# Splitting w_out ahead of attention, loading the first q rows there, and moving two low parts to GpSimd in a Hymba-style encoder layer

## Chip, cores and metric

The kernel runs as one program on one core of a Trainium2 chip. The metric is the device time of one execution in microseconds; a time given for a kernel is the median of its runs.

## The reference

One encoder layer is applied to two sequences of 1024 tokens with model width 1024 (kept as 16 tiles of 128 rows). What matters here, for each sequence:

```python
h = layer_norm(x)
q, k, v, x_lru, y_lru = split(h @ w_in)           # 512, 128, 128, 512, 512 columns
q, k = rope(rms_norm(q)), rope(rms_norm(k))       # 8 query heads and 2 key heads of 64
attn = softmax(q k^T / 8) v                       # full, both directions
lru  = (scan_forward + scan_backward)(conv(x_lru)) * gelu(y_lru)
merged = concat(rms_norm(attn) * attn_out_g, rms_norm(lru) * lru_out_g)
h = layer_norm(alpha * h + merged @ w_out)        # w_out is 1024 x 1024
h = layer_norm(alpha * h + hierarchical_moe(h))   # 16 experts, 2 for each token
```

Everything is float32. The kernel gets float32 accuracy from matrix products by splitting each factor into a high part (rounded to fp32r) and a low part (the rest), and adding three products (`three_pass`, lines 122 to 124).

## The kernel before

There are five stages, each with its own set of semaphores and mostly its own block of five instruction streams: `project_xy`, `qkv_lru`, `attend`, `experts` (with the routing in front) and `combine`. A block ends with a barrier of all engines, and a set of semaphores ends with a clearing and another one (`semaphores`, line 243). Within a block each engine's order is written out by hand; engines meet only in semaphores. The change lies at the end of `qkv_lru` and in the start and the first tile of `attend`.

The end of `qkv_lru` is called the gap here. The projections and scans are over or nearly over, and TensorE (PE) multiplies w_out by the router's columns, so that the router's logits can be had from attention's output: w_out's eight blocks of 128 rows are loaded (SP, lines 886 to 903), each is transposed in pieces on PE (`turn_w`, 953), copied out of PSUM by ScalarE (ACT, `read_w`, 1091) and multiplied by the router's columns (`times_w`, 962); sixteen such steps n, with two buffers at each hand-over. Between them stand the last transposes of q and k (`back`, 987), two column sums of the squared LRU output (`sums`, 923, copied by ACT at 1185), and at the end the product is transposed once more (`turn_r`, 972; `read_r`, 1097; the copy to w_r at 1188). VectorE (DVE) does the last unit's scans and output (1212 to 1222), GpSimd (POOL) the low part of the last q and k rows (`split`, 1316 and 1317).

`attend` loops over 16 tiles of 128 queries, with 8 heads each. For head h, PE transposes the probabilities (1550), computes the scores of head h + 2 (1538, 1539), and after every second head multiplies by v (1564). ACT copies the transposed probabilities to their high part (`d_probs_t_hi`, 1669) and computes exp of head h + 1 (1652). DVE subtracts to get the low part (`d_probs_t_lo`, 1755) and reduces the maximum of head h + 2 (1731). From the second tile on PE also projects the tile before through w_out, in thirds, and the normalisation follows. POOL only applies the layer norm's gain and shift, from the third tile on.

The start of `attend`: SP loads the first two q tiles from DRAM, then the gains out_g, two w_out blocks into the buffers raw, and the rest; ACT makes the high part of v (1645); DVE makes the LRU norms (a chain of small instructions, 1735 to 1738), the first two maxima, then the router part of w_out times out_g (1746) and v's low part (1747). In the first tile each head h also prepares w_out block h: ACT multiplies raw by out_g into `d_wo_hi` (1676), DVE subtracts into `d_wo_lo` (1761), and SP then loads block h + 2 into the freed buffer (1500). The first projection, in tile 1, waits for all of them. In the first tile:

```python
if not post:                                                  # ACT, head
    act.wait_ge(raw_in[h % 2], 16 * (h // 2 + 1))
    act.activation(w_hi[:, h, 0:D], raw[h % 2], ACT.Copy, scale=out_g[:, h:h + 1]).then_inc(hi_made, 1)
if not post:                                                  # DVE, head
    dve.wait_ge(hi_made, h + 1)
    dve.scalar_tensor_tensor(w_lo[:, h, 0:D], raw[h % 2], out_g[:, h:h + 1], w_hi[:, h, 0:D].bitcast(F32), ...)
```

## Time and profile before

| | us |
|---|---|
| median of 3 runs (lowest, highest) | 1601.76 (1598.63, 1602.78) |
| the profiled execution | 1599.9 |
| its span, first to last instruction | 1598.1 |
| PE busy in it | 1444.6 (90%) |
| DVE, ACT, POOL busy | 1126.0, 928.1, 481.1 |
| `project_xy`, to about | 218 |
| `qkv_lru`, to | 485.4 |
| start and first tile of `attend`, to | 529.2 |
| the rest of attention, to about | 1070 |
| routing, experts and the last norm | 1598.1 |

The profile is of one execution, its times count from the span's start. A line number such as L1755 is one of the kernel before. In a timeline row the first number is the start, the second the length, and the bracket at its end the idle time of that engine just before, with what ended it. Several matmuls or activations are merged into one row (x8). PEclk is the granted TensorE clock: 1.00 is 2.4 GHz, 0.50 is 1.2 GHz.

### The profile page before, as it was taken

Reading aid. Unit: us, or ns where it says so; the run is one execution under the profiler, and the core shown is the slowest. Engines: PE = TensorE matmul, PEld = TensorE weight load, DVE = VectorE, ACT = ScalarE, POOL = GpSimd, SP = SyncE. Lnnn points to the kernel's source line nnn. Section 1 sums busy time; section 2 is a strip of 40 time slices with the busy share of each in tenths; the row PEclk is TensorE's granted clock in tenths of the full one; section 3 lists DMA queues with packets and bytes.
Section 4 is the critical chain, followed back from the end, with each engine's and each line's share of the span. In section 5 each row is a group of like instructions: output and inputs, shape, how many; then the busy total and the mean of one; then the engine's idle time right before and its main releaser. Section 6 shows DMA issues by size and latency. Waiting matters only on the chain. (4 is left out here: it accounts for less than half of the span.)

```text
span 1598.1 us, 30295 instructions
## 1 busy us (share of the span) xinstructions
PE 1444.6 (90%) x8945; PEld 1258.7 (79%) x8947; DVE 1126.0 (70%) x2198; ACT 928.1 (58%) x1624; POOL 481.1 (30%) x347
## 2 busy tenths in 40 slices
PE   6999989999996999999999999975899999999940
PEld 5999977777765899999999999963777788777820
DVE  8787547999977888888888888877444334444237
ACT  4444338788776666666666666633565445555325
POOL 1212124565440011111121111131454433555318
PEclk9999999999998999999999999996999999999965
DMA  8865641544454112111112121127798787786576
GB/s 290 297 229 195 231 144 70 192 165 151 166 174 163 52 61 79 60 59 59 61 67 92 65 73 60 47 96 239 230 277 251 205 246 189 216 266 151 110 228 256
DMA packets 126214, 250.09 MB, mean 156 GB/s; under 512 B 24498, under 2 KB 77746, under 8 KB 126132
## 3 DMA queue, kind: packets, MB, share of 16 engines
q1 hardware_dynamic: 94000, 160.97, 29.2%
q0 software_dynamic: 12528, 45.99, 12.3%
q10 hardware_dynamic: 19604, 42.09, 7.0%
q8 instruction: 45, 0.74, 0.2%
q14 instruction: 37, 0.30, 0.1%
HBM read 154.35 MB, written 94.67 MB: 156 GB/s over the span
## 5 line engine op out<-in xcount | busy, mean ns | idle before, releaser
L1755 DVE TENSOR_TENSOR d_probs_t_lo<-d_pt_ps,d_probs_t_hi 128x512 fp32r<-128x512 f32 x256 | 165.0, 686 | 63.6 <-ACT d_probs_t_hi L1669 62.0
L1669 ACT ACTIVATE d_probs_t_hi<-d_pt_ps 128x512 fp32r<-128x512 f32 x256 | 139.2, 596 | 95.6 <-PE d_pt_ps L1550 89.3
L1731 DVE TENSOR_REDUCE d_neg_max<-d_s_ps 128x1 f32<-128x1024 f32 x128 | 155.5, 1215 | 3.4 <-PE d_s_ps L1539 3.4
L122 PE MATMUL acc<-k_hi,wl_hi 128*128 128x256 f32 x512 | 145.8, 285 | 4.4 <-DVE k_lo L597 4.4
L1652 ACT ACTIVATE d_probs<-d_s_ps,d_neg_max 128x1024 f32<-128x1024 f32 x128 | 143.4, 1121 | 4.3 <-DVE d_neg_max L1731 4.3
L122 PE MATMUL e_a_ps<-up_hi,e_xt_hi 128*128 x336 | 137.1, 408 | 9.7 <-DVE e_xt_lo L2591 5.0
L123 PE MATMUL acc<-k_lo,wl_hi 128*128 128x256 f32 x512 | 144.9, 283 | 0.0
L124 PE MATMUL acc<-k_hi,wl_lo 128*128 128x256 f32 x512 | 144.9, 283 | 0.0
L1550 PE MATMUL d_pt_ps<-ident,d_probs 128*128 128x128 f32 x1024 | 132.9, 273 | 4.7 <-ACT d_probs L1652 3.2
L1564 PE MATMUL d_ot_ps<-d_probs_t_hi,d_v_split 128*128 128x256 f32 x512 | 127.4, 287 | 8.3 <-DVE d_probs_t_lo L1755 8.3
L123 PE MATMUL e_a_ps<-up_lo,e_xt_hi 128*128 x336 | 133.4, 397 | 0.0
L124 PE MATMUL e_a_ps<-up_hi,e_xt_lo 128*128 x336 | 132.3, 394 | 0.0
L1564 PE MATMUL d_ot_ps<-d_probs_t_lo,d_v_split 128*128 128x256 f32 x512 | 124.9, 282 | 0.0
L1550 PEld LDWEIGHTS d_pt_ps<-ident,d_probs 128*128 128x128 f32 x1024 | 116.9, 140 | 7.8 <-ACT d_probs L1652 6.5
L122 PE MATMUL d_m_ps<-d_wo_hi,d_m_hi 128*128 128x348 f32 x360 | 120.6, 335 | 0.0
L1538 PE MATMUL d_s_ps<-k_hi,d_q_tile 128*128 128x512 f32 (+1 forms) x256 | 112.0, 438 | 5.5 <-DMA d_q_tile<-q_dram 5.5
L123 PE MATMUL d_m_ps<-d_wo_lo,d_m_hi 128*128 128x348 f32 x360 | 115.8, 322 | 0.0
L124 PE MATMUL d_m_ps<-d_wo_hi,d_m_lo 128*128 128x348 f32 x360 | 115.6, 321 | 0.0
L1929 POOL TENSOR_TENSOR l_h_tile<-d_s_tile,l_ln_g_b 128x512 f32<-128x512 f32 x16 | 20.6, 1285 | 309.6 <-ACT d_s_tile L1702 291.9
L1564 PEld LDWEIGHTS d_ot_ps<-d_probs_t_hi,d_v_split 128*128 128x128 f32 x512 | 97.1, 190 | 15.4 <-issue 15.4
L2416 POOL DMA_INDIRECT xg<-h_dram,ix x43 | 42.1, 978 | 211.5 <-ACT e_yt L2543 119.7
L122 PEld LDWEIGHTS acc<-k_hi,wl_hi 128*128 128x128 f32 x512 | 98.3, 192 | 5.0 <-DVE k_lo L597 5.0
(414 smaller groups left out, 4089.3 us busy)
## 6 DMA issues: line engine op xcount, KB each, us to landing
up_raw<-in_exp_w SPq DMA_DIRECT2D x32, 1024.0 KB, 9.5
down_raw<-in_exp_w SPq DMA_DIRECT2D x16, 1024.0 KB, 14.1
d_h_tile<-h_dram SPq DMA_DIRECT2D x16, 522.0 KB, 4.8
h_dram<-v_all ACTq DMA_DIRECT2D x16, 512.0 KB, 3.2
ht_hi_dram<-k_hi ACTq DMA_DIRECT2D x8, 1024.0 KB, 4.3
ht_lo_dram<-k_lo ACTq DMA_DIRECT2D x8, 1024.0 KB, 6.7
d_q_tile<-q_dram SPq DMA_DIRECT2D x16, 512.0 KB, 4.3
h_dram<-l_h_tile SPq DMA_DIRECT2D x16, 512.0 KB
```

Of the source, the lines that this page charges most:

```text
L122: pe.matmul(out, lhs[0], rhs[0], start=first, stop=False)
L123: pe.matmul(out, lhs[0], rhs[1], start=False, stop=False)
L124: return pe.matmul(out, lhs[1], rhs[0], start=False, stop=last)
L1538: pe.matmul(out, q_t[u][:, h, :], k_hi[:, h // GQ, keys], start=True, stop=False)
L1550: last = pe.transpose(pt_ps[c][:, j, :], pr[h % 2][:, k * P:(k + 1) * P], ident[:])
L1564: last = pe.matmul(ot_ps[:, 0:2 * P], vs[:, s * TPS + k, h // GQ].rearrange("p c d -> p (c d)"), part[:, k].rearrange("p e t -> p (e t)"), ...
L1652: act.activation(pr[h % 2][:], s_ps[h % 2][:], ACT.Exp, bias=nm[:, u, h:h + 1], accum_out=rsum[:, u, h:h + 1]).then_inc(p_done, 1)
L1669: act.activation(pt_hi[:, c * HALF:(c + 1) * HALF, h % 2], pt_ps[c][:], ACT.Copy).then_inc(pth_done[c], 1)
L1731: dve.tensor_reduce(nm[:, u, h:h + 1], s_ps[h % 2][:], AX, ALU.max, negate=True).then_inc(nm_done, 1)
L1755: dve.tensor_tensor(pt_lo[:, part, h % 2], pt_ps[c][:], pt_hi[:, part, h % 2].bitcast(F32), ALU.subtract)\
L1929: pool.tensor_tensor(h1[:, part], s_t[u][:, part], g_b[:, part], ALU.mult).then_inc(hg_done, 1)
L2416: pool.indirect_dma_start(xg[u][:], None, h1_dram, bass.IndirectOffsetOnAxis(ix[u][:, 0:1], 0))\
```

## The change

- Blocks 2 to 7 of w_out (EARLY_W = 6) are split in the gap. ACT makes each high part (`split_w`) between its reads of the transposed pieces, DVE the six low parts after the last output. The parts lie in two tensors that take the place of the q weights of `qkv_lru` (`wo_hi_early`, `wo_lo_early`). The raw blocks 4 to 7 are loaded one by one into buffers that the scans have left (xc, r) instead of a room of their own, and out_g is loaded in `qkv_lru`.
- Blocks 0 and 1 are split in attention's first tile: high part by ACT at heads 1 and 3, low part by POOL in two instructions (gain, subtraction). The router part moves to heads 3 and 4.
- The first two q tiles are loaded in the gap into the place of the gated inputs (`spare`), after the last scans. Their semaphores are made in the outer scope, which ends after `attend` and there has a clearing and a barrier of its own.
- v's low part goes from DVE to POOL. ACT computes one exp of a single column first, so that the table is loaded before v's high part.
- PE waits for the ones only before the router sums, no longer at the block's start.

The diff, cut to its core:

```diff
@@ -153,6 +155,9 @@
...
+            out_g = sb("out_g", [P, KD])
+            ahead = kept.enter_context(semaphores(nc, "q_"))
+            q_in = [ahead(f"q_loaded{u}") for u in range(2)]
...
+                with nc.sbuf_tensor("wo_hi_early", [P, EARLY_W, DW], F32R) as wo_hi_early:
...
+                with ExitStack() as places:
+                    q_t = [places.enter_context(nc.sbuf_tensor(f"q_tile{u}", [P, NQ, P], F32R)) for u in range(2)]
                 spare = sb("spare", [P, 2 * FT * CH + FT])
+                with nc.sbuf_tensor("wo_lo_early", [P, EARLY_W, DW], F32R) as wo_lo_early:
@@ -779,9 +791,10 @@
...
-        wo = wo_early[0::2] + [wo_gates[:, k * D:(k + 1) * D] for k in range(2)] + [wo_late[:, k * D:(k + 1) * D] for k in range(KD - 4)]
+        wo = wo_early[0::2] + [wo_gates[:, k * D:(k + 1) * D] for k in range(2)] + [xc[0][:], xc[1][:], r[0][:, 0], r[0][:, 1]]
+        LATE_W = KD - EARLY_W
         wo_t = wo_early[1::2]
-        WO_LOADS = ((0, 1), (1, 2), (2, 4), (4, 6), (6, KD))
@@ -858,10 +873,14 @@
...
+            def load_w(k):
+                sp.dma_start(wo[k], rows[:, k, :]).then_inc(wo_in[k if k < 2 else k - 1], 16)
...
+            with nc.allow_non_contiguous_dma("small per-feature vectors"):
+                for n, gain in enumerate(gains):
+                    sp.dma_start(out_g[:, n * FT:(n + 1) * FT], gain[0].rearrange("(f p) -> p f", p=P)).then_inc(out_g_in, 16)
@@ -883,30 +905,31 @@
...
                 if g == NU - 1:
-                    for n, (a, b) in enumerate(WO_LOADS):
-                        if b <= 2:
-                            sp.wait_ge(pj_done, NT - 1)
-                            dst = wo[a]
-                        elif b <= 4:
-                            sp.wait_ge(gates_done, GH * NU)
-                            dst = wo_gates[:, (a - 2) * D:(b - 2) * D]
-                        else:
-                            continue
-                        sp.dma_start(dst.rearrange("p (k n) -> p k n", n=D), rows[:, a:b, :]).then_inc(wo_in[n], 16)
+                    sp.wait_ge(pj_done, NT - 1)
+                    load_w(0)
+                    load_w(1)
+                    sp.wait_ge(gates_done, GH * NU)
+                    sp.dma_start(wo_gates.rearrange("p (k n) -> p k n", n=D), rows[:, 2:4, :]).then_inc(wo_in[2], 16)
                     store(NU - 2)
-                    sp.wait_ge(pj_done, NT)
-                    for n, (a, b) in enumerate(WO_LOADS):
-                        if a >= 4:
-                            sp.dma_start(wo_late[:, (a - 4) * D:(b - 4) * D].rearrange("p (k n) -> p k n", n=D), rows[:, a:b, :])\
-                              .then_inc(wo_in[n], 16)
+                    sp.wait_ge(ix_done, NU - 1)
+                    load_w(4)
+                    load_w(6)
+                    sp.wait_ge(ix_done, NU)
+                    load_w(5)
                     load_y(NU - 1)
                     continue
...
+                if g == NU:
+                    sp.wait_ge(last_sums, 1)
+                    load_w(7)
+                    sp.wait_ge(scans_done, NU)
+                    sp.wait_ge(q_stored, 16 * (TILES.index(1) + 1))
+                    for u in range(2):
+                        sp.dma_start(q_ahead[u][:].rearrange("p h t -> p (h t)").bitcast(F32), q_dram[u]).then_inc(q_in[u], 16)
@@ -1095,6 +1118,10 @@
...
+            def split_w(k):
+                act.wait_ge(wo_in[k if k < 3 else k - 1], 16)
+                act.activation(wo_hi[:, k - LATE_W, 0:D], wo[k], ACT.Copy, scale=out_g[:, k:k + 1]).then_inc(wo_hi_made, 1)
@@ -1175,14 +1202,23 @@
             read_w(10)
             read_r(0)
             split(NT - 1)
-            for n in range(11, 15):
-                read_w(n)
+            act.wait_ge(out_g_in, 32)
+            read_w(11)
+            split_w(2)
+            read_w(12)
+            split_w(3)
+            read_w(13)
+            split_w(4)
+            read_w(14)
             evict_q(NT - 1)
             read_w(15)
             evict_k(NT - 1)
             squares_of_output(NU - 1)
+            split_w(5)
+            split_w(6)
             act.wait_ge(last_sums, 2)
             act.activation(lru_sums[:, NU - 2:NU, :], pj[1][:, SUMS:SUMS + 2 * TPS].rearrange("p (n c) -> p n c", c=TPS), ACT.Copy)
+            split_w(7)
             read_r(1)
@@ -1275,6 +1311,10 @@
...
+            for k in range(LATE_W, KD):
+                dve.wait_ge(wo_hi_made, k - LATE_W + 1)
+                dve.scalar_tensor_tensor(wo_lo[:, k - LATE_W, 0:D], wo[k], out_g[:, k:k + 1], wo_hi[:, k - LATE_W, 0:D].bitcast(F32),
+                                         ALU.mult, ALU.subtract)
@@ -1354,36 +1394,42 @@
...
+        LATE_W = KD - EARLY_W
+        w_hi_late = sb("wo_hi", [P, LATE_W, DW], F32R)
+        w_lo_late = sb("wo_lo", [P, LATE_W, DW], F32R)
+        w_hi = [w_hi_late[:, k] for k in range(LATE_W)] + [w_hi_early[:, k] for k in range(EARLY_W)]
+        w_lo = [w_lo_late[:, k] for k in range(LATE_W)] + [w_lo_early[:, k] for k in range(EARLY_W)]
+        BY_HEAD = {1: 0, 3: 1}
@@ -1482,12 +1527,8 @@
...
             sp.sem_inc(h1_stored, 32)
-            load_q(0, 0)
-            load_q(1, 1)
...
-                for k in range(2):
+                for k in range(LATE_W):
                     sp.dma_start(raw[k], w_out[0, k * P:(k + 1) * P, :]).then_inc(raw_in[k], 16)
...
-            for k in range(2, KD):
-                sp.wait_ge(lo_made, k - 1)
-                sp.dma_start(raw[k % 2], w_out[0, k * P:(k + 1) * P, :]).then_inc(raw_in[k % 2], 16)
@@ -1526,8 +1564,6 @@
...
         def _(pe):
-            pe.wait_ge(ones_made, 2)
@@ -1591,6 +1627,7 @@
...
+                pe.wait_ge(ones_made, 2)
@@ -1611,7 +1648,7 @@
...
-                        pe.wait_ge(lo_made, KD)
+                        pe.wait_ge(lo_made, LATE_W)
@@ -1642,7 +1679,7 @@
...
-            act.activation(vs[:, :, :, 0], v_all[:].rearrange("p t (g d) -> p t g d", g=NKV), ACT.Copy).then_inc(vh_made, 1)
+            act.activation(warm[:], ident[:, 0:1], ACT.Exp)
@@ -1669,14 +1706,14 @@
...
-                if not post:
...
-                    act.wait_ge(raw_in[h % 2], 16 * (h // 2 + 1))
-                    act.wait_ge(out_g_in, 32)
-                    act.activation(w_hi[:, h, 0:D], raw[h % 2], ACT.Copy, scale=out_g[:, h:h + 1]).then_inc(hi_made, 1)
-                    if h == 1:
-                        act.wait_ge(wg_made, 1)
-                        act.activation(w_hi[:, :, D:], w_rg[:], ACT.Copy).then_inc(rh_made, 1)
+                if not post and h in BY_HEAD:
+                    k = BY_HEAD[h]
+                    act.wait_ge(raw_in[k], 16)
+                    act.activation(w_hi[k][:, 0:D], raw[k], ACT.Copy, scale=out_g[:, k:k + 1]).then_inc(hi_made, 1)
+                if not post and h == 4:
+                    act.wait_ge(wg_made, 1)
+                    act.activation(w_hi_late[:, :, D:], w_rg[:, 0:LATE_W], ACT.Copy)
+                    act.activation(w_hi_early[:, :, D:], w_rg[:, LATE_W:], ACT.Copy).then_inc(rh_made, 1)
@@ -1705,7 +1742,11 @@
...
-            run_heads(act, lambda: exp(0, 0, 0), head, aux)
+            def first():
+                act.activation(vs[:, :, :, 0], v_all[:].rearrange("p t (g d) -> p t g d", g=NKV), ACT.Copy).then_inc(vh_made, 1)
+                exp(0, 0, 0)
...
+            run_heads(act, first, head, aux)
@@ -1741,11 +1782,6 @@
...
-                dve.wait_ge(vh_made, 1)
-                dve.wait_ge(out_g_in, 32)
-                dve.tensor_tensor(w_rg[:], w_r[:], out_g[:].unsqueeze(2).broadcast_to([P, KD, RW]), ALU.mult).then_inc(wg_made, 1)
-                dve.tensor_tensor(vs[:, :, :, 1], v_all[:].rearrange("p t (g d) -> p t g d", g=NKV),
-                                  vs[:, :, :, 0].bitcast(F32), ALU.subtract).then_inc(vl_made, 1)
@@ -1757,12 +1793,13 @@
...
-                    dve.wait_ge(hi_made, h + 1)
-                    dve.scalar_tensor_tensor(w_lo[:, h, 0:D], raw[h % 2], out_g[:, h:h + 1], w_hi[:, h, 0:D].bitcast(F32),
-                                             ALU.mult, ALU.subtract).then_inc(lo_made, 1)
-                    if h == 1:
+                    if h == 3:
+                        dve.tensor_tensor(w_rg[:], w_r[:], out_g[:].unsqueeze(2).broadcast_to([P, KD, RW]), ALU.mult).then_inc(wg_made, 1)
+                    if h == 4:
...
-                        dve.tensor_tensor(w_lo[:, :, D:], w_rg[:], w_hi[:, :, D:].bitcast(F32), ALU.subtract).then_inc(rl_made, 1)
+                        dve.tensor_tensor(w_lo_late[:, :, D:], w_rg[:, 0:LATE_W], w_hi_late[:, :, D:].bitcast(F32), ALU.subtract)
+                        dve.tensor_tensor(w_lo_early[:, :, D:], w_rg[:, LATE_W:], w_hi_early[:, :, D:].bitcast(F32), ALU.subtract)\
+                           .then_inc(rl_made, 1)
@@ -1930,6 +1967,14 @@
...
+            pool.wait_ge(vh_made, 1)
+            pool.tensor_tensor(vs[:, :, :, 1], v_all[:].rearrange("p t (g d) -> p t g d", g=NKV),
+                               vs[:, :, :, 0].bitcast(F32), ALU.subtract).then_inc(vl_made, 1)
+            for k in range(LATE_W):
+                pool.wait_ge(hi_made, k + 1)
+                pool.tensor_scalar(raw[k], raw[k], out_g[:, k:k + 1], None, ALU.mult).then_inc(gained, 1)
+                pool.wait_ge(gained, k + 1)
+                pool.tensor_tensor(w_lo[k][:, 0:D], raw[k], w_hi[k][:, 0:D].bitcast(F32), ALU.subtract).then_inc(lo_made, 1)
...

```

## Rows read from the trace of the kernel before

**Rows 1.** Windows: us, busy (PE, PEld, DVE, ACT, POOL), PEclk, DMA share, GB/s

```profile
529.20:1070.00 540.80, 535.04 (x3726) 505.05 (x3723) 455.55 (x942) 347.38 (x706) 75.29 (x59) 1.00 0.19 63
```

**Rows 2.** Waits of PE, 485.4 to 529 us: total, times, longest

```profile
PE d_s_ps L1538 <- DMA d_q_tile<-q_dram: 5.5, 1, 5.5
PE d_ot_ps L1564 <- DVE d_probs_t_lo L1755: 4.4, 3, 1.6
```

**Rows 3.** Timeline from the boundary to the first exp: start us, us, engine

```profile
485.40 1.91 ACT L1645 ACTIVATE d_v_split<-v_all 128x2048 fp32r<-128x2048 f32 x1 [1.10 <-PEq L253]
485.41 0.17 DVE L1719 MEMSET d_ones<- 128x128 f32 x1 [13.91 <-PEq L253]
...
488.44 0.18 DVE L113 SCALAR_TENSOR_TENSOR d_lru_rstd<-d_lru_tmp,d_lru_rstd 128x16 f32<-128x16 f32 x1
...
489.46 0.77 PE L1538 MATMUL d_s_ps<-k_hi,d_q_tile 128*128 128x512 f32 x1 [5.50 <-DMA d_q_tile<-q_dram]
...
491.62 1.23 DVE L1731 TENSOR_REDUCE d_neg_max<-d_s_ps 128x1 f32<-128x1024 f32 x1 [3.00 <-PE d_s_ps L1539]
...
492.88 1.11 ACT L1652 ACTIVATE d_probs<-d_s_ps,d_neg_max 128x1024 f32<-128x1024 f32 x1 [4.27 <-DVE d_neg_max L1731]
```

**Rows 4.** Timelines of PE, ACT and DVE in the first tile, by time

```profile
495.81 1.12 ACT L1652 ACTIVATE d_probs<-d_s_ps,d_neg_max 128x1024 f32<-128x1024 f32 x1
...
497.63 1.16 PE L1550 MATMUL d_pt_ps<-ident,d_probs 128*128 128x128 f32 x8 [1.47 <-DVE d_probs_t_lo L1755]
...
498.30 1.14 ACT L1669 ACTIVATE d_probs_t_hi<-d_pt_ps 128x512 fp32r<-128x512 f32 x2 [0.25 <-PE d_pt_ps L1550]
...
511.79 1.04 PE L1550 MATMUL d_pt_ps<-ident,d_probs 128*128 128x128 f32 x8
...
513.46 1.12 ACT L1652 ACTIVATE d_probs<-d_s_ps,d_neg_max 128x1024 f32<-128x1024 f32 x1
...
514.55 1.16 ACT L1676 ACTIVATE d_wo_hi<-l_s_tile,d_out_g 128x1024 fp32r<-128x1024 f32 x1
...
514.72 1.09 PE L1550 MATMUL d_pt_ps<-ident,d_probs 128*128 128x128 f32 x8 [0.75 <-ACT d_probs L1652]
...
515.60 1.09 ACT L1669 ACTIVATE d_probs_t_hi<-d_pt_ps 128x512 fp32r<-128x512 f32 x2
...
515.74 1.28 DVE L1761 SCALAR_TENSOR_TENSOR d_wo_lo<-l_s_tile,d_out_g,d_wo_hi 128x1024 fp32r<-128x1024 f32 x1 [0.20 <-ACT d_wo_hi L1676]
...
517.34 1.28 DVE L1755 TENSOR_TENSOR d_probs_t_lo<-d_pt_ps,d_probs_t_hi 128x512 fp32r<-128x512 f32 x2
...
518.16 0.36 PE L1564 MATMUL d_ot_ps<-d_probs_t_hi,d_v_split 128*128 128x256 f32 x1 [1.42 <-DVE d_probs_t_lo L1755]
...
520.15 1.04 PE L1550 MATMUL d_pt_ps<-ident,d_probs 128*128 128x128 f32 x8
```

**Rows 5.** Timeline of ACT at a table load in the gap

```profile
446.72 1.28 ACT L1132 ACT_TABLE_LOAD   x1
448.01 1.92 ACT L1132 ACTIVATE lru_th<-lru_th 128x2048 f32<-128x2048 f32 x1
```

**Rows 6.** Waits of ACT, 471 to 477 us

```profile
ACT w_out_rows L1091 <- PE gp L953: 3.0, 3, 1.1
```

**Rows 7.** Waits of ACT, 471 to 484 us

```profile
ACT lru_sums L1185 <- PE pj L923: 2.1, 1, 2.1
ACT lru_th L1097 <- PE pj L962: 0.8, 1, 0.8
```

**Rows 8.** POOL's groups in the later tiles, and its line 1317

```profile
L1929 POOL TENSOR_TENSOR l_h_tile<-d_s_tile,l_ln_g_b 128x512 f32<-128x512 f32 x16 | 20.6, 1285 | 309.6 <-ACT d_s_tile L1702 291.9 <-ACT d_s_tile L1715 17.7
...
L1317 POOL TENSOR_TENSOR k_st<-wq_raw,k_st x16: 719/2705/2790, 255.0 to 472.6; 128x256 fp32r<-128x256 f32 x16
```

**Rows 9.** Windows of one microsecond, columns as in rows 1

```profile
483.00:484.00 1.00, 0.61 (x4) 0.50 (x4) 0.00 (x0) 0.29 (x2) 0.00 (x0) 0.50 0.00 0
...
493.00:494.00 1.00, 0.19 (x1) 0.00 (x0) 0.77 (x1) 1.00 (x2) 0.00 (x0) 0.98 1.00 376
```

More of the change, by code:

```diff
@@ L78 @@
 EARLY = 6
+EARLY_W = 6
 class Chain:
@@ L200, in build @@
             h1_stored = sem("h1_stored")
-            attend(nc, sem, w_out, attn_out_g, lru_out_g, ln1_g, ln1_b, router_bg, router_be, r_w, w_r, ident, k_hi, k_lo, v_all, lru_dram, lru_sums, h_dram, q_dram, h1_dram, sum_dram,
+            attend(nc, sem, q_t, q_in, w_out, out_g, wo_hi_early, wo_lo_early, ln1_g, ln1_b, router_bg, router_be, r_w, w_r, ident, k_hi, k_lo, v_all, lru_dram, lru_sums, h_dram, q_dram, h1_dram, sum_dram,
                    logits, s_last, h1, gain, shift, mv, rr, h1_stored)
@@ L737, in qkv_lru @@
         GH = 2 * NG
[L738 removed]
+        hr, k_st, g_b, (ss, ms, tmp, rs) = small_rooms
         gtab = sb("rope_gain", [P, 2, TPS, 2, HD])
@@ L863, in store @@
                 sp.dma_start(unit(lru_dram, n), ys[:]).then_inc(lru_stored, 16)
+            rows = w_out[0].rearrange("(k p) n -> p k n", p=P)
             load_x(0)
@@ L1331, in need, with attend @@
         eng.wait_ge(sem, value)
-def attend(nc, sem, w_out, attn_g, lru_g, ln_g, ln_b, router_bg, router_be, r_w, w_r, ident,
+def attend(nc, sem, q_t, q_in, w_out, out_g, w_hi_early, w_lo_early, ln_g, ln_b, router_bg, router_be, r_w, w_r, ident,
            k_hi, k_lo, v_all, lru_dram, lru_sums, h_dram, q_dram, h1_dram, sum_dram, logits,
@@ L1356, in attend @@
         BACK = 2 * P
-        w_hi = sb("wo_hi", [P, KD, DW], F32R)
-        w_lo = sb("wo_lo", [P, KD, DW], F32R)
+        vs = sb("v_split", [P, NT, NKV, 2, HD], F32R)
+        pr = [sb(f"probs{j}", [P, SEQ]) for j in range(2)]
+        sb("place_of_w_hi", [P, EARLY_W * DW])
+        o_sum = sb("o_sum", [P, PAIRS, 2, HD])
+        ot = sb("o_t", [P, 2 * P])
+        ones = sb("ones", [P, P])
+        ssa = sb("ssa", [P, 1])
+        sb("place_of_q_tiles", [P, 2 * NQ * P])
+        var = sb("vars", [P, 2])
+        sb("place_of_w_lo", [P, EARLY_W * DW])
+        pt_hi = sb("probs_t_hi", [P, TPS, 2, P], F32R)
+        pt_lo = sb("probs_t_lo", [P, TPS, 2, P], F32R)
+        o_n = sb("o_n", [P, QW])
+        junk = sb("junk", [P, QW])
+        yt = sb("lru_tile", [P, FT, P])
+        m_hi = sb("m_hi", [P, KD, P], F32R)
+        LATE_W = KD - EARLY_W
[4 more added lines that the diff above has]
+        BY_HEAD = {1: 0, 3: 1}
         w_rg = sb("w_out_router_gain", [P, KD, RW])
-        out_g = sb("out_g", [P, KD])
         rb_b = sb("router_b", [P, RW])
@@ L1363, in attend @@
         r_off = sb("router_offset", [P, RW])
-        ones = sb("ones", [P, P])
-        vs = sb("v_split", [P, NT, NKV, 2, HD], F32R)
-        q_t = [sb(f"q_tile{u}", [P, NQ, P], F32R) for u in range(2)]
-        pr = [sb(f"probs{j}", [P, SEQ]) for j in range(2)]
-        pt_hi = sb("probs_t_hi", [P, TPS, 2, P], F32R)
-        pt_lo = sb("probs_t_lo", [P, TPS, 2, P], F32R)
-        ot = sb("o_t", [P, 2 * P])
         nm = sb("neg_max", [P, 2, NQ])
@@ L1381, in attend @@
         rl = sb("lru_rstd", [P, NT])
-        m_hi = sb("m_hi", [P, KD, P], F32R)
         m_lo = sb("m_lo", [P, KD, P], F32R)
-        ssa = sb("ssa", [P, 1])
-        var = sb("vars", [P, 2])
+        warm = sb("exp_warm", [P, 1])
         tmp = sb("tmp_a", [P, 2])
@@ L1409, in attend @@
         lo_made = sem("wo_lo_made")
-        q_in = [sem(f"q_loaded{u}") for u in range(2)]
+        gained = sem("wo_raw_gained")
         s_done = sem("scores_done")
```

21 lines of the change are left out of this document (9 added, 12 removed).

## The prediction

> **What bounds the kernel now.** I read the windows by stage first. Attention's later tiles (529.2 to 1070 us) keep TensorE (PE) busy 535.0 of 540.8 us [rows 1]. The reader is to see that from 529.2 on PE alone sets the pace, so that a microsecond gained ahead of it is carried to the end. Next PE's waits in the first tile and the start before it: 5.5 us for the first q rows, and 4.4 us in three pairs of heads for VectorE's (DVE) d_probs_t_lo [rows 2]. Last the timelines: the boundary between the two blocks [rows 3], the pairs of heads [rows 4], and the end of the block before [rows 5 to 7], which I call the gap.
>
> **The change part by part.** The sum is made against the profiled execution: 1598.1 us of span in 1599.9 us. The runs shown have a median of 1601.76 us, 1.9 us above it; I subtract the gain from that median.
>
> *The start, q rows.* Now PE starts at 489.46, 4.1 us after the block, when q has landed; DVE's first maximum starts at 491.62 and the first exp at 492.88, 7.48 us after ScalarE (ACT) began the block at 485.40, which I call the start [rows 3]. In the change the two q tiles are issued after the last scans (about 469), so PE can start with the block. What is late next is DVE: its chain of LRU norms ends at 488.44 + 0.18 = 488.62, 3.22 after the start, in both kernels. The first two products of scores need four matmuls each; the first four end before that even at half clock. So the first maximum comes at start + 3.25, the first exp 1.26 later (491.62 to 492.88) at start + 4.51 instead of + 7.48: **2.97 us gained**. ACT must be free by then: the new exp table warm-up is first, then v's high part. A table load takes 1.28 us and the activation behind it follows at once (446.72, 448.01) [rows 5], so 1.28 + 0.2 + 1.91 = 3.4 us after the start, 1.1 us before exp. The Trainium skill ("ScalarE: Activation LUTs", What ACT_TABLE_LOAD costs) speaks of 2.66 us for a switch, drain included; by that estimate ACT would be free at + 4.8, and exp 0.3 us later. The trace shows no such drain behind its load.
>
> *v's low part on GpSimd (POOL).* On DVE it stood ahead of d_probs_t_lo of head 0, for which PE waited 1.47 us before the transposes at 497.63 [rows 4]. Without that wait the transposes of head 1 follow its exp (495.81) by 1.26, as those of head 5 do (513.46, 514.72), at 497.07: **0.56 us gained** in the first pair. The later part of that pair is PE's own work (scores, the router sums, the products with v). On POOL the instruction has 2048 elements per partition. A 512-element one takes 1.285 us there while DVE reads PSUM beside it, so 5.1 us; a 256-element one takes 0.72 us alone but 2.7 in half the cases [rows 8], namely where DVE works on two SBUF inputs, a factor of 3.76, so 19.4 us at worst. I take 5.1: beside it DVE computes maxima and low parts of PSUM data. It starts at start + 3.4 and ends at + 8.5; PE needs it at the product of head 1, which I put at start + 12.4 (exp + 1.26 for head 0's transposes, 2.93 to head 1's as from 511.79 to 514.72, 2.03 for these and scores, and the 1.7 of the router sums). It is hidden unless it takes over 9.0 us. The Trainium skill ("GPSIMD Engine Reference", Specifications) says that GpSimd's SBUF interfaces are shared with VectorE and contended by instructions with two SBUF inputs or in a two-port mode; the two sizes of rows 8 agree. By that rule v's low part stays near 5 us, and the price falls in the gap instead, where the new low splits meet GpSimd's split of the last tile.
>
> *Six w_out blocks out of the first tile.* A pair of heads takes 511.79 to 520.15 = 8.36 us [rows 4]. Follow the odd head: its transposes start at 514.72; their first half lets ACT begin d_probs_t_hi 0.67 later (497.63, 498.30), at 515.4, where d_wo_hi now holds it until 515.60. DVE begins d_probs_t_lo at 517.34, since d_wo_lo (from 515.74) and the pair's small sums stand before it, 1.60 us, 0.40 of them the sums. Without the w_out splits DVE can begin some 0.6 behind ACT (half of ACT's 1.09 and a hand-over), at 516.04; it was free at 515.54 (before its 0.20 of idle), so the sums end at 515.94 and don't hold it. The product with v follows 0.82 later, at 516.86 instead of 518.16; PE's scores end at 516.75, since it idles 1.42 us before that product. So 1.3 us per pair, and PE's wait shrinks to 0.11. The three waits together are 4.4 us [rows 2]; less three times 0.11 that is **4.1 us gained**. ACT's two remaining high splits come in heads 1 and 3 behind the exp, 1.05 us each in time in which ACT waits for the product. The router part moves to heads 3 and 4: two small activations and two small subtractions, by d_wo_lo's rate some 0.35 us on DVE ahead of the pair's sums: **0.2 us lost**. POOL's low parts of blocks 0 and 1 (two instructions of 1024 elements each, at 1.285 us per 512 5.1 us a block) are due at tile 1's first projection, over 10 us later; at the contended rate 19 us a block would be too late, which counts with the rival below. Each d_wo transfer that SP issued in the tile goes away; the first two loads and the norm rows come 1.5 to 2 us earlier in SP's queue.
>
> *The gap, ACT.* Six high splits of 1.05 us (514.55 to 515.60) [rows 4]. Three stand before three reads of transposed w_out, ahead of which ACT idles 3.0 us in sum, 1.1 the longest [rows 6]: 0.1 us late each at most, absorbed by PE's double buffering. Two stand in the 2.1 us of idle before the copy of lru_sums: they fit. The sixth has 0.8 us of idle before the read of the router part [rows 7] and takes 1.05: **0.25 us lost**. At the worst none is hidden: 6.3 us. *DVE* idles for 13.91 us before the block [rows 3]; six low splits of 1.2 us lie there, the last one behind ACT's last split, which I put at 483.0, until 484.3; ACT's own end, 1.10 before the block's start, moves to 484.55. *SP*: the loads go into buffers that are already free and land 4 us later, well before 464 and 470 where their transposes read them; block 7 waits for the first last_sums (463), q for the scans (469), both ahead of the last LRU store (471.5), whose issue they don't delay; that store then lands up to 4 us later, by 480.
>
> *One thing more in the diff.* The q semaphores live in the outer scope, whose end after attention clears them and adds a barrier of all engines, on DVE's path into the routing. Not shown by itself; from the boundary between the blocks, where two barriers and a clearing take 1.10 us of ACT [rows 3], it lies between 0 and 1.1; I take **0.5 us lost**, about half.
>
> *The clock.* PE's granted clock is 0.50, the lower level (1.2 GHz), from 483 to 493: it fell while PE did narrow sums and transposes with waits, and rose at 493 after the eight matmuls of scores from 489.46 on [rows 9]. In the change these matmuls run from 485.7 to about 489.1, and then PE waits 2.3 us for exp. If the rise has come by then, nothing is lost; if the lower clock lasts through the first pair, transposes and products take twice as long, 0.8 + 1.7 + 1.9 us at the most on the path, some 4.4. I take **0.7 us lost**, near the lower end since the same eight matmuls raised it here.
>
> Sum: 2.97 + 0.56 + 4.1 - 0.2 - 0.25 - 0.5 - 0.7 = 6.0 us. Predicted 1601.8 - 6.0 = 1595.8 us.
>
> **The rivals.**
> 1. *The first pair at low clock.* For it: the 2.3 us hole behind the scores; against: PE's waits of 1.5 us in this tile left the clock up. It costs 4.4 in place of 0.7: 1599.5 us.
> 2. *The gap isn't free.* ACT's splits stand in line with PE's transposes of w_out, and GpSimd's split of tile 15 is slowed by DVE's low splits, so the block ends later by up to the 6.3 us of splits less my 0.25: 1601.8 at the end of that range, 1599 at half. For it: ACT's idle pieces fit to within 0.1 us each; against: the buffers on PE's side.
> 3. *GpSimd's v is late, the slower side.* The first product with v waits for vl_made; behind it on PE's queue is all of attention. At 19.4 us it would be ready at start + 22.8, 10.4 us after PE wants it: 1595.8 + 10.4 = 1606.2 us. It decides from 9.0 us on, and the kernel is slower than before from 15.0 us. Against: in the later tiles the same engine runs at 1.285 us per 512 beside the same DVE work.
> 4. *Less is taken out than said*: another wait takes the place of DVE's in the pairs (the score matmuls end only 0.11 us earlier than the new start), half of the 4.1 us: 1597.9 us.
>
> **How the numbers follow.** The forecast has 0.60, rival 1 0.12, rival 2 0.11, rival 3 0.06, rival 4 0.11. I call faster or slower what lies over 0.3% (4.8 us) from 1601.8, about what a measurement of this kernel can tell from no change. The bound 1597.0 is 1.2 us above my forecast: the forecast case falls below it some 8 times in 10, with a clock that rises at once (1595.1) and the barrier at its lower end (1594.6) on one side, rival 4's on the other; small parts of the others too, 0.63 in all. Slower is rival 3 and the tail of rival 2, 0.08. Same 0.29. The range goes from 1592.0 (no clock or barrier loss, and a pair or two gaining more at PE's bound, 2.6 us more) to 1600.5 (rivals 1, 4 and half of 2).
>
> **What would show it.** In the changed profile: PE's wait for d_q_tile gone; the first exp about 4.5 us after the start; the start at 485.65 (within 0.4); pairs of heads 7.1 us apart in the first tile; PE's wait for d_probs_t_lo under 1 us in sum; v's low part on GpSimd near 5 us; the first tile ending 7 us earlier; and nearly the same 541 us from there to attention's end. It would be wrong if the block starts over 1 us later, if PE waits for GpSimd, or if granted clock 0.50 lasts beyond 491.

## The result and the profile after

The changed kernel takes 1605.45 us (median of 20 runs, 1601.56 to 1611.69), the kernel before, in the same session, 1600.59 us (1598.54 to 1606.44). The ratio is 1.0027 with a 95% interval of 1.0016 to 1.0038. I had forecast 1595.8 us. So the kernel became 4.9 us slower where 6.0 us were to be gained. In a second session (e1) it was 2.6 us slower by the medians. One of the twelve runs of e14 took 7177 us and is left out of its median and its ratio. The profiled execution after is the slowest of the 20 (span 1609.9 us), which the second trace of the same kernel (e1) helps to judge.

The stretch that the change was aimed at, the boundary and the first tile of attention, did become shorter. Timeline of ScalarE (ACT), after, from the boundary on (start us, us, engine, line, operation; in brackets the idle time before it):

```profile
492.08 1.28 ACT L1682 ACT_TABLE_LOAD   x1 [1.10 <-PEq L265]
493.38 0.20 ACT L1682 ACTIVATE d_exp_warm<-ident 128x1 f32<-128x1 f32 x1
493.49 1.89 ACT L1746 ACTIVATE d_v_split<-v_all 128x2048 fp32r<-128x2048 f32 x1
...
496.62 1.11 ACT L1689 ACTIVATE d_probs<-d_s_ps,d_neg_max 128x1024 f32<-128x1024 f32 x1 [1.24 <-DVE d_neg_max L1772]
...
499.03 0.60 ACT L1706 ACTIVATE d_probs_t_hi<-d_pt_ps 128x512 fp32r<-128x512 f32 x1 [1.21 <-PE d_pt_ps L1586]
...
509.01 1.09 ACT L1706 ACTIVATE d_probs_t_hi<-d_pt_ps 128x512 fp32r<-128x512 f32 x2
...
516.14 1.09 ACT L1706 ACTIVATE d_probs_t_hi<-d_pt_ps 128x512 fp32r<-128x512 f32 x2
...
524.68 1.09 ACT L1706 ACTIVATE d_probs_t_hi<-d_pt_ps 128x512 fp32r<-128x512 f32 x2
...
531.82 0.60 ACT L1706 ACTIVATE d_probs_t_hi<-d_pt_ps 128x512 fp32r<-128x512 f32 x1
```

The start is at 492.08, and the first exp follows at 496.62, 4.54 us later, in place of 7.48 [rows 3]. The copies of the third, fifth, seventh and ninth head (509.01, 516.14, 524.68, 531.82) mark the pairs of heads: 7.13, 8.54 and 7.14 us, where before they took 8.54, 8.36 and 8.35 (the second is the one in [rows 4]). What I call the first pair runs from the first exp to the third head's copy, 12.39 us here and 11.07 before. The waits of TensorE (PE) in this stretch, after (total, times, longest):

```profile
PE d_pt_ps L1586 <- ACT d_probs L1689: 4.3, 4, 2.1
PE d_ot_ps L1600 <- DVE d_probs_t_lo L1791: 2.0, 3, 1.6
PE d_s_ps L1574 <- PEq L265: 1.4, 1, 1.4
```

The wait for the q rows is gone, and of the 4.4 us for d_probs_t_lo 2.0 are left [rows 2]. From the start to the ninth copy it is 39.74 us instead of 43.80 (485.40 [rows 3] to 529.20, where the steady state of [rows 1] begins).

The loss lies where nothing was edited. The first DMA issue of the second block, `qkv_lru`, before and after:

```profile
222.47 0.33 SPq L853 DMA_DIRECT2D xc<-xc_dram  x1
```

```profile
228.06 0.33 SPq L868 DMA_DIRECT2D xc<-xc_dram  x1
```

So `project_xy`, whose code is the same, ends 5.6 us later. Two windows of PE in it (us, busy and count, granted clock, DMA share, GB/s), before and after:

```profile
0.00:20.00 20.00, 4.39 (x18) 1.00 0.91 327
...
100.00:150.00 50.00, 50.00 (x433) 1.00 0.64 226
```

```profile
0.00:20.00 20.00, 4.48 (x18) 1.00 0.91 310
...
100.00:150.00 50.00, 50.00 (x422) 1.00 0.60 211
```

PE is "busy" 50 of 50 us in both, at the same granted clock, yet does 422 matmuls instead of 433. The busy time hides this; only the count tells. The weight loads (groups of PEld, 100 to 200 us; count, busy, mean ns), before and after, are fewer too, and each is 4 ns longer:

```profile
L124 PEld LDWEIGHTS acc<-k_hi,wl_lo 128*128 128x128 f32 x266 | 50.0, 188 | 0.0
```

```profile
L126 PEld LDWEIGHTS acc<-k_hi,wl_lo 128*128 128x128 f32 x259 | 49.7, 192 | 0.0
```

The length of a load doesn't tell the pace, though. In e16 (below) the same group takes 187 ns, less than before, and 50 us hold 422 matmuls.

```profile
L124 PEld LDWEIGHTS acc<-k_hi,wl_lo 128*128 128x128 f32 x259 | 48.5, 187 | 0.0
```

The change puts out_g, 32 bytes per partition, into the outer scope behind lru_sums, and every buffer of this block that is allocated after it moves by 32 bytes. That this shift costs the time is theory A, which the experiments test. The addresses below are worked out from the order and sizes of the allocations; no trace shows them.

### The profile page after: what moved, and what is told of

Read it like the earlier page. It is cut to its first block and busy times, and to the rows that moved or that the text cites. A ratio compares the mean times of both kernels' runs of the same rounds, so it can differ in the third digit from the quotient of the medians.

```text
span 1609.9 us, 30303 instructions
## 1 busy us (share of the span) xinstructions
PE 1458.0 (91%) x8946; PEld 1267.9 (79%) x8947; DVE 1127.7 (70%) x2196; ACT 928.7 (58%) x1626; POOL 500.2 (31%) x352
## 5 line engine op out<-in xcount | busy, mean ns | idle before, releaser
L1574 PE MATMUL d_s_ps<-k_hi,q_tile 128*128 128x512 f32 (+1 forms) x256 | 113.4, 443 | 1.4 <-PEq L265 1.4
L1575 PE MATMUL d_s_ps<-k_lo,q_tile 128*128 128x512 f32 (+1 forms) x256 | 102.9, 402 | 0.0
L125 PEld LDWEIGHTS acc<-k_lo,wl_hi 128*128 128x128 f32 x512 | 99.6, 195 | 0.0
L126 PEld LDWEIGHTS acc<-k_hi,wl_lo 128*128 128x128 f32 x512 | 99.6, 195 | 0.0
```

The source lines that it names most:

```text
L125: pe.matmul(out, lhs[0], rhs[1], start=False, stop=False)
L126: return pe.matmul(out, lhs[1], rhs[0], start=False, stop=last)
L1574: pe.matmul(out, q_t[u][:, h, :], k_hi[:, h // GQ, keys], start=True, stop=False)
L1575: last = pe.matmul(out, q_t[u][:, h, :], k_lo[:, h // GQ, keys], start=False, stop=True)
```

## The experiments

Stages of the traces, in us. "Block 1" ends at the first DMA issue of `qkv_lru`, "block 2" at its first turned piece of w_out, "gap" at attention's start, "first tile" at the ninth copy, "tiles" at the last copy, "routing" at the experts' first weight load, "experts" at their last (loads of `up_hi`), and the rest is the end of the span.

| kernel | block 1 | block 2 | gap | first tile | tiles | routing | experts | rest |
|---|---|---|---|---|---|---|---|---|
| before | 222.5 | 227.3 | 35.67 | 43.80 | 523.7 | 57.6 | 409.7 | 77.9 |
| after | 228.1 | 227.3 | 36.76 | 39.74 | 524.5 | 58.4 | 416.9 | 78.3 |
| e1 after again | 227.9 | 226.9 | 36.1 | 38.4 | 524.5 | 57.3 | 416.8 | 78.4 |
| e4 one set | 226.9 | 228.0 | 35.8 | 38.6 | 524.5 | 57.2 | 409.1 | 78.3 |
| e5 after, +256 B | 222.5 | 228.2 | 36.9 | 39.5 | 525.4 | 57.3 | 410.0 | 78.1 |
| e9 router at head 6 | 222.6 | 227.3 | 35.8 | 36.4 | 525.4 | 58.0 | 414.7 | 77.9 |
| e11 all mended | 221.8 | 228.3 | 36.9 | 36.4 | 525.4 | 56.8 | 409.8 | 77.6 |
| e13 five matmuls | 221.6 | 227.2 | 35.9 | 36.4 | 525.4 | 57.2 | 408.6 | 78.3 |

The experts' stage is untouched and takes 408.6 to 416.9 us in single traces, of either kernel's kind (415.7 in e6, a variant of the kernel before). It makes most of the spread of the whole times, so effects of one or two microseconds are read from the stages, not from a total. PE after, some 86 us into that stage (a timeline row, then a window):

```profile
1200.55 0.79 PE L124 MATMUL e_a_ps<-up_hi,e_xt_hi 128*128 x1 [2.04 <-issue]
```

```profile
1200.70:1203.70 3.00, 3.00 (x8) 0.50 1.09 371
```

PE pauses for 2 us at this place in seven of the 18 traces of this document (after, e1, e6, e9, e10, e14, e15), and in all of these but e10 the granted clock then is at 0.50 for 3.4 to 6.8 us (3.4 in after). These six are the six longest experts' stages, 412.6 to 416.9 us, against 408.6 to 412.0 for the other twelve. In after, the stage is 3.6 us behind the kernel before soon after the pause. Why PE pauses there is open; the profile names nothing that it waited for. It came in six of eleven traces of the changed kernel and its variants and in one of seven of the kernel before and its own, too few to say that the change makes it more frequent.

**e1, the changed kernel once more.**

> The changed kernel once more, for a second trace of it. In its first trace the untouched first block (project_xy) ends 5.6 us later than before, with 422 matmuls of 128x256 per 50 us instead of 433 at the same granted clock, and the experts' block takes some 7 us more. Theory A (addresses: the 32 bytes of out_g shift every later buffer by half of 64 bytes, and TensorE's operands with them): both recur, q's first load about 228 us. Theory V (that execution happened to be a slow one; it took 1611.7 us where the median is 1605.5): the first block is back at about 222.5 us, and the experts' block within 2 us of before's.

Median 1605.25 us; ratio to before 1.0012 (0.9994 to 1.0029). Block 1 is 227.9 us with 422 matmuls again: for that stage theory V falls. The experts took 416.8 us again, with the pause.

**e2, the kernel before with 32 bytes more.**

```diff
             lru_sums = sb("lru_sums", [P, SEQS * FT, TPS])
+            sb("pad", [P, KD])
```

> The kernel before with 32 unused bytes per partition behind lru_sums, where the change puts out_g; nothing else. Theory A: the first block is 5 to 6 us longer and the kernel takes 1606 to 1612 us. Theory V: 1600.6 us as before, within 1.

1610.44 us, ratio 1.0048 (1.0026 to 1.0069). Windows of PE in e2:

```profile
0.00:20.00 20.00, 4.43 (x18) 1.00 0.96 312
...
100.00:150.00 50.00, 50.00 (x422) 1.00 0.59 213
```

Nothing but the addresses differs, and block 1 has both of its losses, the pace (422 matmuls) and the loads of the first 20 us (312 GB/s for 327): it ends at 226.9 us (+4.4, for 5 to 6 expected). Theory A holds for block 1. The experts' stage took 409.8 us in this trace, without the 7 us more of the changed kernel.

**e3, the changed kernel, shifted by 64 bytes.** The edit is a second `sb("pad", [P, KD])` behind out_g.

> The changed kernel with 32 unused bytes more behind out_g, so that every later buffer is shifted by 64 bytes instead of 32. Theory A: 5 to 6 us faster than the changed kernel, 1599 to 1600 us. Theory V: 1605.5 us as the changed kernel, within 1.

1600.66 us, ratio 0.9991 (0.9975 to 1.0007); block 1 225.7 us, 428 matmuls. The direction was right, the size in that stage half of what I expected (2.4 us). The whole time is 4.6 us below e1's of the same session, more than this stage explains.

**e4, without the added barrier.** The q semaphores come from attention's own set `d_`, made earlier.

> The changed kernel with the two q semaphores in attention's own set, made earlier, so that the clearing and the barrier of all engines at the end of attention are not added. My prediction priced them at 0.5 us (0 to 1.1). Theory that this step was sized right: 0.5 us faster than the changed kernel, at most 1.1. Rival: that barrier meets the stores of attention's last rows and costs 1.6 us, what the trace shows lost between the first tile and the first expert.

1602.83 us, ratio 0.9991 (0.9975 to 1.0008). Routing as a whole scatters (56.7 to 60.1 us in the 18 traces), but its first part doesn't. From the start of the last two copies of `d_probs_t_hi` in attention to the first weight load of the routing's counts (`e_a_ps<-r_busy,r_ones`), it takes 30.64 to 30.68 us in the seven traces with the added clearing and barrier, 30.23 or 30.24 in the four of the changed kernel without them (e4, e11, e13, e14), and 30.09 to 30.14 in the kernel before and its variants. After, then e4 (copies, weight load):

```profile
1055.79 1.08 ACT L1706 ACTIVATE d_probs_t_hi<-d_pt_ps 128x512 fp32r<-128x512 f32 x2 [0.82 <-PE d_pt_ps L1586]
1086.46 0.12 PEld L2271 LDWEIGHTS e_a_ps<-r_busy,r_ones 128*128 128x128 bf16 x1 [0.31 <-issue]
```

```profile
1053.29 1.09 ACT L1705 ACTIVATE d_probs_t_hi<-d_pt_ps 128x512 fp32r<-128x512 f32 x2 [0.83 <-PE d_pt_ps L1585]
1083.52 0.13 PEld L2270 LDWEIGHTS e_a_ps<-r_busy,r_ones 128*128 128x128 bf16 x1 [0.31 <-issue]
```

So the barrier costs 0.4 us up to there; my 0.5 was right, and the rival's 1.6 is not seen. The whole time says less: it is 2.4 us below e1's of the same session, and only 0.4 of that is the barrier.

**e5, the changed kernel, shifted by 256 bytes.**

```diff
             out_g = sb("out_g", [P, KD])
+            sb("pad", [P, 56])
```

> The changed kernel with 224 unused bytes behind out_g: every later buffer of the first blocks is shifted by 256 bytes, so that its address modulo 256 is that of the kernel before. e2 showed that 32 bytes alone cost the first block 4.4 us (433 to 422 matmuls per 50 us), e3 that a shift of 64 leaves 428. Theory A1 (what matters is an address modulo 256 or a divisor of it): 433 matmuls per 50 us, the block ends at 222 to 223 us, the whole 5 us faster than the changed kernel, 1600 us or less. Rival A2 (only shifts by a larger power of two, or none, give the old pace): 422 to 428 matmuls per 50 us and 1603 to 1605 us.

1599.37 us, ratio 0.9985 (0.9969 to 1.0001), against 1.0027 for the change: 0.4%, some 6 to 7 us. Block 1 is back at 222.5 us with 433 matmuls, and A1 holds. The stage shows it, not the whole time: e4, whose buffers are still at the 32 bytes, came to 0.9991, and the intervals of e4 and e5 overlap.

**e6 and e7, which buffers.** Both are the kernel before. In e6 only wl_hi and wl_lo have another place modulo 256, in e7 all later buffers but these two (and 32 bytes ahead of all).

```diff
+        sb("pad_before", [P, 8])     # e7: [P, 56]
         w_hi = sb("wl_hi", [P, KD, NF * P], F32R)
         w_lo = sb("wl_lo", [P, KD, NF * P], F32R)
+        sb("pad_behind", [P, 56])    # e7: [P, 8]
```

> The kernel before with 32 unused bytes ahead of wl_hi and 224 behind wl_lo: of all buffers only these two, the weights that TensorE loads in the first block, have another address modulo 256 (128 in place of 96); the moving operands k_hi and k_lo are at 128 in every kernel. Theory B (the weight load and the moving operand meet where both addresses agree modulo 256): 422 matmuls per 50 us, the block ends near 227 us. Rival C (DMAs or the other engines' buffers do it): 433 and 222.5 us.

> The complement of e6: all later buffers of the first block are shifted by 32 bytes, wl_hi and wl_lo alone keep 96 modulo 256. Theory B: 433 matmuls per 50 us and 222.5 us. Rival C: 422 and 227 us.

Windows of PE in e6, then in e7:

```profile
0.00:20.00 20.00, 4.45 (x18) 1.00 0.96 330
...
100.00:150.00 50.00, 50.00 (x422) 1.00 0.61 223
```

```profile
0.00:20.00 20.00, 4.49 (x21) 1.00 0.95 311
...
100.00:150.00 50.00, 50.00 (x432) 1.00 0.62 219
```

The two halves separate. The address of the weights alone changes the matmuls' pace (block 1: 225.5 us, +3.0). The other buffers alone slow the loads at the block's start, 311 GB/s instead of 327, and this block ends at 223.8 us (+1.3). Neither theory had the second part: C was wrong on the pace, B left 1.3 us out. The later tiles of attention take 525.6 us in e7 and 525.5 in e2, against 523.6 to 523.8 in the kernels before whose other buffers are at their old place (before, e6, e8, e12, e16): addresses cost there as well, 1.9 us.

The loads' part resembles a rule of the Trainium skill ("DMA: Bandwidth & Descriptors", How a descriptor splits into AXI transactions): a descriptor that doesn't start at a multiple of 256 bytes fetches from the multiple below, and the unused bytes still cost transfer time. That rule is told of what is read, and here it is the destination in SBUF that moved, so no run shows that it is the cause. What the traces show is the cost: where the raw weights begin at 0 modulo 256 the first 20 us move 325 to 331 GB/s (12 traces), and at 32 or 64 (after, e1 to e4, e7) 310 to 313.

**e8, e12, e16, other addresses of the weights.** As e6, with 160, 128 and 192 bytes ahead and the rest of 256 behind.

> The kernel before with wl_hi and wl_lo at 0 modulo 256 (96 before), all others as before. Theory B with a distance of 128 bytes to the moving operand: at least 433 matmuls per 50 us, perhaps a few more; the block ends at 222.5 us or up to 4 us earlier. If what counts is the address modulo 64 alone (96 and 32 good, 0 and 128 bad): 422 and 227 us.

> The kernel before with wl_hi and wl_lo at 224 modulo 256. So far 96 gives 433 matmuls per 50 us, 160 gives 428, 0 gives 424 and 128 gives 422, with the moving operands at 128. If an odd multiple of 32 is what is good (96 and 160 modulo 64 are 32, 0 and 128 are 0): 428 or more. If it is the distance to the moving operand (32 and 32 from it for 96 and 160, 128 for 0, 0 for 128): 224 is 96 away and I expect 424 to 428.

> The kernel before with wl_hi and wl_lo at 32 modulo 256. Known so far: 0 gives 424 matmuls per 50 us, 96 433, 128 422, 160 428, 224 426 or 427. If odd multiples of 32 are good: at least 426, as 224. If only the distance to the moving operands (at 128) counts, in either direction alike, 32 is as far as 224: 426 or 427. Below 425 both fall.

The paces by address, with before, e6 and, for 160, e3:

| wl_hi, wl_lo modulo 256 | 0 | 32 | 96 | 128 | 160 | 224 |
|---|---|---|---|---|---|---|
| matmuls per 50 us | 424 | 422 | 433 | 422 | 428 | 426 to 427 |

The moving operands stand at 128 in each. e8 gave 424 where theory B had 433 or more. e12 gave 426 to 427, within what the distance to the moving operands asked for and a little under the 428 of an odd multiple of 32; I let both stand. 32 (e16) gave 422, at which both fall. What rule orders these numbers is open; that the kernel before stood at the best of the six addresses tried is shown. The whole times of the single runs were 1608.57 (e6), 1606.70 (e7), 1604.84 (e8), 1605.75 (e12) and 1604.49 us (e16).

**e9, the router subtractions two heads later.** In the timeline of VectorE (DVE) after, first, and GpSimd (POOL), second:

```profile
519.10 1.56 DVE L1800 TENSOR_TENSOR d_wo_lo<-d_w_out_router_gain,d_wo_hi 128x40 fp32r<-128x40 f32 x1
520.58 0.27 DVE L1801 TENSOR_TENSOR wo_lo_early<-d_w_out_router_gain,wo_hi_early 128x120 fp32r<-128x120 f32 x1
521.17 1.27 DVE L1791 TENSOR_TENSOR d_probs_t_lo<-d_pt_ps,d_probs_t_hi 128x512 fp32r<-128x512 f32 x2
```

```profile
495.46 4.52 POOL L1971 TENSOR_TENSOR d_v_split<-v_all,d_v_split 128x2048 fp32r<-128x2048 f32 x1 [15.57 <-ACT d_v_split L1746]
...
518.24 2.37 POOL L1977 TENSOR_TENSOR d_wo_lo<-l_h_tile,d_wo_hi 128x1024 fp32r<-128x1024 f32 x1
```

```diff
-                    if h == 4:
+                    if h == 6:
                         dve.wait_ge(rh_made, 1)
```

> e5 with VectorE's two router subtractions behind head 6 instead of head 4. In e5 the first of them (128x40) takes 1.56 us and ends with GpSimd's subtraction of block 1 (513.61 to 515.98), and that pair of heads takes 8.54 us where the others take 7.14. Theory D (VectorE's instruction on two SBUF inputs waits until GpSimd's two-input one is through): behind head 6 GpSimd is idle, the instruction takes under 0.3 us, all three later pairs take 7.14 us, and the first tile ends 1.4 us earlier than in e5. Rival (these subtractions cost 1.4 us wherever they stand): the fourth pair takes 8.5 us instead and the tile's end doesn't move.

DVE in e9:

```profile
517.90 0.19 DVE L1801 TENSOR_TENSOR d_wo_lo<-d_w_out_router_gain,d_wo_hi 128x40 fp32r<-128x40 f32 x1
518.01 0.28 DVE L1802 TENSOR_TENSOR wo_lo_early<-d_w_out_router_gain,wo_hi_early 128x120 fp32r<-128x120 f32 x1
```

0.19 us in place of 1.56, and the three pairs take 7.14, 7.14 and 7.17 us. Theory D holds: the instruction on 40 elements takes 1.55 to 1.59 us in all seven traces that have it at head 4, and 0.19 in the four that have it at head 6. In the trace above it ends at 520.66, just behind POOL's subtraction (518.24 + 2.37 = 520.61). The Trainium skill ("GPSIMD Engine Reference", Specifications) says that the two share their SBUF interfaces, with contention when VectorE reads two inputs from SBUF, and this trace agrees: 1.56 us beside POOL, 0.19 without.

In e9 the clock also happened to rise early, shortly before 490, 4 us after attention's start, so that the first pair took 10.44 us. Whole time of the one run 1599.88 us.

**e10, matmuls that nobody reads.** Three ahead of the last sums, four around the router part's last transposes, and in attention:

```diff
+                for _ in range(5):
+                    pe.matmul(m_ps[:], q_t[0][:, 0, :], k_hi[:, 0, 0:512], start=True, stop=True)
```

> e5 with matmuls of 128x512 that nobody reads on TensorE: three ahead of the last sums, one and three around the last transposes of the router part, five behind the first scores of attention. In e5 the granted clock is 0.50 from 482 to 499. Theory E (the low clock comes from TensorE's narrow and waiting work there, and costs the first pair 1.7 us and the gap 1.2): the clock stays 1.00 through the boundary, the gap shrinks to 35.7 us, the first pair from exp to the third head's copy is 10.5 us instead of 12.2, and the first tile ends 2.5 us earlier than in e5. Rival (the clock falls anyway; the added work only delays): no gain, or up to 1 us lost.

Half right. The clock fell in the gap anyway (0.71 in 480 to 482, 0.50 until 491), and ACT waited 2.34 us at the barrier instead of 1.10, behind the last three matmuls. But it was up again at 491, and the first pair took 10.43 us. The gap was 37.7 us, not 35.7, the first tile 37.8 us against 39.5 in e5. Whole time of the one run 1598.36 us.

**e11, all of it together.**

> e5, e9, e10 and e4 (no added barrier) in one kernel. If the theories hold they add up: first tile 3.9 us earlier than in e5, 0.1 to 0.8 us from the barrier, so some 4 us faster than e5's 1599.4 and 5 to 6 faster than the kernel before, about what I had predicted of the change. If the time of the later blocks varies as it did so far (409 to 417 us for the experts in single traces), the median of the runs still moves by 3 to 5 us.

1596.55 us, ratio 0.9976 (0.9961 to 0.9991): faster than the kernel before by 3.8 us by the ratio (4.9 by the session's medians), not the 5 to 6. The first tile is 36.4 us; the gap's matmuls cost 1.0 to 1.1.

**e13 and e14, with five and with no unread matmuls.** e13 is e11 without the seven in the gap.

> e11 without the seven unread matmuls in the gap; the five behind the first scores of attention stay. In e11 and e10 the gap was 36.9 and 37.7 us, with ScalarE waiting 2.3 us at the barrier, where the others wait 1.1. Theory: the three behind the last transposes (1.65 us at the low clock) held the barrier and kept nothing up; the gap is 35.8 us again and the whole about 1 us faster than e11 (1596.5 us), the clock back at 1.00 some 5 us after attention's start. Rival: the gap's matmuls let the clock rise sooner; then the first pair takes 12 us instead of 10.4 and the kernel is 1 us slower than e11.

> e13 without its five unread matmuls as well. Theory: in the wait of 2.1 us behind the scores the clock's rise is missed in part of the executions (e5: low until 499, first pair 12.2 us; e9: up at 489, 10.4 us), so the median is 0.5 to 1.5 us above e13's. Rival: TensorE's eight matmuls of scores alone decide, and the two kernels take the same time within 0.3 us.

e13: 1597.51 us, ratio 0.9978 (0.9962 to 0.9995), gap 35.9, first pair 10.44. e14: 1598.02 us, ratio 0.9971 (0.9956 to 0.9987), gap 35.8, first pair 11.35. The stages come as expected, but the times of e11, e13 and e14 can't be told apart. Windows of PE at the boundary (clock in the third number), e13, then e14:

```profile
488.00:490.00 2.00, 1.53 (x6) 0.93 0.86 300
490.00:492.00 2.00, 1.57 (x11) 1.00 0.55 156
492.00:494.00 2.00, 1.09 (x8) 1.00 1.02 410
494.00:496.00 2.00, 2.00 (x17) 1.00 0.56 229
```

```profile
488.00:490.00 2.00, 1.80 (x5) 0.53 0.82 279
490.00:492.00 2.00, 0.14 (x1) 1.00 0.89 280
492.00:494.00 2.00, 2.00 (x12) 0.83 0.57 171
494.00:496.00 2.00, 1.48 (x7) 0.50 0.96 392
```

In e14 the clock rose behind the scores, and after PE's nearly idle stretch from 490 to 492 fell again to 0.50 (1.2 GHz) in the middle of the first pair. In e13, whose start is 1.4 us earlier, the five matmuls fill that stretch (PE busy 1.53 of 2 us), and it stayed. The first pair took 10.43 or 10.44 us in all three traces with the five matmuls (e10, e11, e13).

**e15, v's low part on DVE.** e5 with the instruction moved back.

> e5 with v's low part back on VectorE, behind the first two maxima and ahead of the first low part of the probabilities. It takes some 2.2 us there, until 6.5 us after the start, and the copy of the first transposed probabilities comes at 5.5. Theory: the first low part of the probabilities starts up to 1 us later, the first pair is 0.6 us longer than with the same clock in e5 (12.8 with the low clock, 11.0 with the high one). Rival: nothing, since at the low clock TensorE is late anyway: 12.2.

Inconclusive. It took 2.28 us and the copy waited nowhere else, but the clock differed from e5's (up at 488, down from 492 to 495): first pair 11.19 us, within the 10.4 to 12.4 that the clock alone makes. Whole time of the one run 1602.15 us.

## Why the prediction was wrong, step by step

- **The step that failed is one the sum did not have.** I argued that a microsecond gained ahead of 529.2 is carried to the end, and took all code that the diff doesn't touch to keep its time. Yet the diff of the allocations stood there: out_g in the outer scope moves every later buffer by 32 bytes. That costs 5.4 to 5.6 us in block 1 of the changed kernel's two traces (4.4 in e2, where nothing else is changed, 4.5 in e4, nothing in e5). The sum has no such term, and it takes back nearly all of a gain of 6.0. The rest is in the first tile, which gave 4.1 us where my terms for it add up to 6.7 (the clock and the router part, below), and in the gap, the tiles and the routing.
- *Start, -2.97.* Right: 4.54 us from the start to the first exp, for 4.51 forecast; -2.94. ACT was free 1.2 us ahead (forecast 1.1).
- *v's low part, -0.56; rival 3.* 4.52 us on POOL (estimate 5.1), and PE never waited for it. At the high clock the first pair takes 10.43 or 10.44 us (e9, e10, e11, e13) in place of 11.07 (492.88 to 503.95 before), -0.63. The size fits, but the same pair also lost the splits of two w_out blocks and the router part, and e15 doesn't tell them apart; that it is v's low part isn't shown. The kernel did come out slower, as rival 3 had it, but not by that mechanism.
- *Six blocks out of the first tile, -4.1, and router part, +0.2.* In e9 the three pairs take 21.45 us instead of 25.25 (503.95 to 529.20): -3.8 for -3.9. As the change was made they took 22.81 us: the router subtraction met POOL's second block, and cost 1.4 us where I had 0.2. I had weighed only what DVE does to POOL (1.285 us "beside the same DVE work"), not what POOL does to DVE.
- *The gap, +0.25; rival 2.* 35.8 to 35.9 us in e3, e4, e9, e13, e14 and e15, 35.7 to 35.8 in six of the seven kernels without the splits (36.4 in e12): they are hidden, +0.1. The 36.1 to 36.9 of after, e1 and e5 come in part of the traces: the last product of w_out runs at the lower clock, wholly in after and e5 (1.89 us) and in part in e1 (1.49), where it takes 1.04 us before.
- *The added barrier, +0.5.* Right: 0.4 us (e4), read ahead of the part of the routing that scatters.
- *The clock, +0.7; rival 1.* In after it stays at 0.50 through the first pair, where it was 0.98 at 493 before [rows 9]: 12.39 us. Over seven traces without the five matmuls (e15 left out) the first pair takes 10.44 to 12.39, mean 11.56: +1.1. My "same eight matmuls" raised it only in part of the executions. Rival 1 came true in the profiled one, in part: 2.0 us, not 4.4. It showed my own sign of being wrong, a clock of 0.50 beyond 491, but this is the smaller part of the miss.
- *The steady tiles.* 524.3 to 524.5 us (after, e1, e3, e4) and 525.4 (the seven traces with 256 bytes) for 523.7 before, +0.6 to +1.7; e2 and e7 show that addresses alone can do 1.9 there. Not separated further, and missing in the sum as well.

Sum by stages for after: 5.6 + 1.1 - 4.1 + 0.8 + 0.8 = +4.2 up to the experts, near the 4.9 of the medians. The experts' 7 us more come on top in both traces of this kernel, which are slower than its median. They go with PE's pause and the lower clock behind it; e4 and e5, with the same code there and no pause, took 409 and 410. What makes the pause stays open.

## What to carry to other kernels

A small tensor in an outer scope is an edit of everything allocated behind it: give it a room that shifts nothing, or pad it to 256 bytes, before its real effect is judged. The padding restored block 1 here, though not all: attention's later tiles took 525.4 us with it and 524.3 to 524.5 without. Compare the count of matmuls per window in stages that weren't edited, since busy time and granted clock were the same while PE was 2.6% slower. And when work moves to GpSimd, look at each two-input VectorE instruction that can fall beside it: here a tiny one waited out the rest of GpSimd's.
